# mLSTM stage of a hybrid encoder step: the decay mask as one product for four heads, the row values in two parts, and an end in which ScalarE normalizes while VectorE alternates two jobs

## The reference, cut to what matters

```
# per block of tokens and head: b = cumsum(log_sigmoid(f)), causal mask
dmat  = where(causal, b[t] - b[s] + ig[s], -inf)
m_t   = max(b + m, max_s dmat)
wqk   = exp(dmat - m_t) * (q @ k.T)                    # pair weights
num   = s_inter * (q @ c) + wqk @ v;  den likewise
h     = num / max(|den|, exp(-m_t))
c_new = s_old * c + (wg * k).T @ v                     # state, an output
# behind it, per token and head
hc    = (h - mean(h)) * rsqrt(var(h) + eps)            # headwise LayerNorm
yc    = hc * ml_norm_g * sigmoid(o)
```

## Time and profile before

| what | value |
|---|---|
| median of three runs | 2857.32 us (2831.56, 2857.32, 2858.39) |
| profiled execution | 2832.34 us |
| its span | 2830.6 us |
| TensorE busy in the span | 2560.8 us, 90% |
| VectorE, ScalarE, GpSimd busy | 1594.4, 1332.7, 649.7 us |
| `stage_mlstm` in the span | from 842.8 us; the next stage's first transfer is issued at 952.29 us |

### The profile page before, as it was taken

One profiled execution on the slowest core, in us unless ns is written; L12 is line 12 of the kernel. 1 busy time (PEld: TensorE's weight loads), 2 busy tenths in 40 slices (PEclk: granted clock), 3 DMA queues, 4 the chain that ended last, 5 costly groups with the idle time before them and its releaser, 6 DMA issues. The chain is left out here.

```text
span 2830.6 us, 40715 instructions
## 1 busy us (share of the span) xinstructions
PE 2560.8 (90%) x15168; PEld 2301.0 (81%) x15168; DVE 1594.4 (56%) x2533; ACT 1332.7 (47%) x2070; POOL 649.7 (23%) x508
## 2 busy tenths in 40 slices
PE   5999698998889699999989889699999999999990
PEld 4998597897658599999987567599999999999990
DVE  4564331216656644444534365577777777777774
ACT  3665420215433333434332222377777767777762
POOL 4000110004202001011113223134333343343333
PEclk8999899999999799999999889799999999999995
DMA  6120222213274655565534312689898898898964
GB/s 196 47 55 26 91 77 88 90 49 119 83 288 122 132 132 149 145 163 135 141 100 154 118 44 69 198 273 273 245 277 264 259 276 250 268 274 252 272 192 159
DMA packets 390447, 463.27 MB, mean 164 GB/s; under 512 B 21661, under 2 KB 314645, under 8 KB 390330
## 3 DMA queue, kind: packets, MB, share of 16 engines
q1 hardware_dynamic: 369160, 395.81, 45.4%
q0 software_dynamic: 16832, 55.62, 8.2%
q10 hardware_dynamic: 4338, 10.23, 0.9%
HBM read 397.62 MB, written 63.98 MB: 163 GB/s over the span
## 5 line engine op out<-in xcount | busy, mean ns | idle before, releaser
L3102 PE MATMUL banks<-slot_rowsT,expert_w_high 128*128 128x384 f32 x2048 | 604.2, 363 | 0.2 <-issue 0.2
L3104 PE MATMUL banks<-slot_rowsT,expert_w_low 128*128 128x192 f32 x2048 | 515.4, 252 | 0.0
L3104 PEld LDWEIGHTS banks<-slot_rowsT,expert_w_low 128*128 128x128 f32 x2048 | 392.9, 192 | 1.3
L3102 PEld LDWEIGHTS banks<-slot_rowsT,expert_w_high 128*128 128x128 f32 x2048 | 386.1, 189 | 2.0 <-issue 0.6
L3138 ACT CAST expert_w_high<-expert_w 128x2048 fp32r<-128x2048 f32 x128 | 238.1, 1910 | 20.5 <-DMA expert_w<-in_exp_w 20.5
L3197 DVE TENSOR_TENSOR expert_w_low<-expert_w,expert_w_high 128x2048 fp32r<-128x2048 f32 x96 | 216.7, 2284 | 20.8 <-ACT expert_w_high L3138 20.8
L3007 POOL TENSOR_TENSOR expert_w_low<-expert_w,expert_w_high 128x2048 fp32r<-128x2048 f32 x32 | 147.7, 4615 | 273.7 <-ACT expert_w_high L3138 273.7
L2050 PE MATMUL banks<-xT_chunk_high,w_gates_high 128*128 128x384 f32 x576 | 193.5, 336 | 15.0 <-DVE xT_chunk_low L2118 15.0
L2051 PE MATMUL banks<-xT_chunk_low,w_gates_high 128*128 128x384 f32 x576 | 193.2, 335 | 0.0
L2052 PE MATMUL banks<-xT_chunk_high,w_gates_low 128*128 128x384 f32 x576 | 193.1, 335 | 0.0
L3263 DVE TENSOR_TENSOR expert_w_low<-expert_w,expert_w_high 128x1024 fp32r<-128x1024 f32 x128 | 157.5, 1231 | 54.0 <-ACT expert_w_high L3167 54.0
(11 more groups left out here) (494 smaller groups left out, 6164.9 us busy)
## 6 DMA issues: line engine op xcount, KB each, us to landing
expert_w<-in_exp_w SPq DMA_DIRECT2D x128, 1024.0 KB, 8.9
expert_w<-in_exp_w SPq DMA_DIRECT2D x32, 2048.0 KB, 10.9
w_gates<-in_w_in SPq DMA_DIRECT2D x72, 512.0 KB, 4.5
cached_k<-in_cache_sb_k SPq DMA_DIRECT2D x16, 1024.0 KB, 8.3
cached_v<-in_cache_sb_v SPq DMA_DIRECT2D x16, 1024.0 KB, 9.9
w_proj<-in_w_pa SPq DMA_DIRECT2D x24, 512.0 KB, 5.1
w_ax_ag<-in_w_in SPq DMA_DIRECT2D x16, 512.0 KB, 5.1
w_ml_piece<-in_w_in SPq DMA_DIRECT2D x24, 256.0 KB, 4.0
```

Source lines behind the costliest of these rows:

```text
L3102: nc.tensor.matmul(out[:, 0:2 * SLOTS], hi, xgT[:, par, k].rearrange("p a s -> p (a s)"), start=(k == 0), stop=(k == DT - 1), skip_group_c ...
L3104: last = nc.tensor.matmul(out[:, 0:SLOTS], lo, xgT[:, par, k, 0, :], start=False, stop=(k == DT - 1), skip_group_check=True)
```

## The change

Four things change, all in `stage_mlstm`.

1. The mask. The causal masks are laid out once for four heads (`masks`, 128 x 512) in the one-pass type F32R, the identity is copied to that type too, and one product of 512 columns writes the mask of all heads into bank 0.
2. The row values. `m.w` is split into a high part (rows 0 to 3 of `w_rows`) and the remainder (rows 32 to 35), the selector is copied to both places, and one one-pass product of 36 rows per head adds both parts.
3. What that needs first: two clearing operations and a subtraction on VectorE, six copies on ScalarE, and waits of TensorE's first product for them.
4. The end. The normalization is ScalarE's (scale `rstd`, bias `shift` = -mean * rstd); variance and eps come before the requests' states; VectorE alternates a request's state and a tile's o gate, and TensorE alternates a request's products and a tile's transposes, in steps `s`, the gate and the transposes three steps behind.

```diff
+        w_rows = sb("w_row_parts", [L, T], F32R)              # L = 32 + H
+        sel = sb("head_selector_parts", [L, H, P], F32R)
+        ident = sb("ident_one_pass", [P, P], F32R)
+        masks = sb("causal_by_head", [P, 2, H, P], F32R)
...
         # TensorE, scores(i)
+                else:
+                    pe.wait_ge(masks_ready, 3)
+                    pe.wait_ge(parts_ready, 1)
+                nc.tensor.matmul(g.bank[0][:], ident[:], mask.rearrange("p h t -> p (h t)"), start=True, stop=False,
+                                 skip_group_check=True)
                 for h in range(H):
-                    out = g.bank[0][:, h * P:(h + 1) * P]
-                    nc.tensor.matmul(out, g.sel[:, h, :], m.w[:, cols], start=True, stop=False)
-                    last = nc.tensor.matmul(out, g.ident[:], mask[:], start=False, stop=True)
+                    last = nc.tensor.matmul(g.bank[0][:, h * P:(h + 1) * P], sel[:, h, :], w_rows[:, cols],
+                                            start=False, stop=(h == H - 1), skip_group_check=True)
...
         # TensorE, the end (request_state(b) is the loop body of before, turn_yc(i) the transposes)
+            for s in range(NT + 3):
+                if s < NB:
+                    request_state(s)
+                if s >= 3:
+                    turn_yc(s - 3)
...
         # ScalarE, first
+            act.wait_ge(parts_zero, 2)
+            for lo in (0, 32):
+                nc.scalar.copy(sel[lo:lo + H], g.sel[:])
+            nc.scalar.copy(w_rows[0:H], m.w[:]).then_inc(parts_high, 1)
+            nc.scalar.copy(ident[:], g.ident[:]).then_inc(masks_ready, 1)
+            for a, mask in enumerate((g.causal, g.causal_s)):
+                nc.scalar.copy(masks[:, a], mask[:].unsqueeze(1).broadcast_to([P, H, P])).then_inc(masks_ready, 1)
...
         # ScalarE, the end (move_yc(i) waits for yc_turned and copies to ycT, as before)
+            act.wait_ge(std_ready, 2)
+            for i in range(NT):
+                for h in range(H):
+                    part = hc[:, i, h * P:(h + 1) * P]
+                    last = nc.scalar.activation(part, part, ACT.Identity, bias=shift[:, i, h, :],
+                                                scale=rstd[:, i, h, :])
+                last.then_inc(hat_ready, 1)
+                if i >= 3:
+                    move_yc(i - 3)
...
         # VectorE, first; the old clearing of m.qz stands between these two and the subtraction
+            nc.vector.memset(sel[:].bitcast(F32), 0.0).then_inc(parts_zero, 1)
+            nc.vector.memset(w_rows[:].bitcast(F32), 0.0).then_inc(parts_zero, 1)
...
+            dve.wait_ge(parts_high, 1)
+            nc.vector.tensor_tensor(w_rows[32:32 + H], m.w[:], w_rows[0:H].bitcast(F32), ALU.subtract
+                                    ).then_inc(parts_ready, 1)
...
         # VectorE, the end
+            def gate_rows(i):
+                dve.wait_ge(hat_ready, i + 1)
...
+            for s in range(NT + 3):
+                if s == 1:
+                    dve.wait_ge(std_ready, 1)
+                    link(nc.vector.reciprocal(rstd[:], rstd[:]))
+                    nc.vector.scalar_tensor_tensor(out=shift[:], in0=mv[:, :, :, 0:1], scalar=-1.0, in1=rstd[:],
+                                                   op0=ALU.mult, op1=ALU.mult).then_inc(std_ready, 1)
+                if s < NB:
+                    request_state(s)
+                if s >= 3:
+                    gate_rows(s - 3)
```

More of the change, by code:

```diff
@@ L1640, in stage_mlstm, with sb @@
         sem = ctx.enter_context(stage_semaphores(nc))
-        def sb(name, shape):
-            return ctx.enter_context(nc.sbuf_tensor(name, shape, F32))
+        def sb(name, shape, dt=F32):
+            return ctx.enter_context(nc.sbuf_tensor(name, shape, dt))
+        L = 32 + H
+        w_rows = sb("w_row_parts", [L, T], F32R)
+        sel = sb("head_selector_parts", [L, H, P], F32R)
+        ident = sb("ident_one_pass", [P, P], F32R)
+        masks = sb("causal_by_head", [P, 2, H, P], F32R)
+        parts_zero = sem("r_parts_zero")
+        parts_high = sem("r_parts_high")
+        parts_ready = sem("r_parts_ready")
+        masks_ready = sem("r_masks_ready")
+        hat_ready = sem("r_hat_ready")
         c_state = sb("c_state", [P, 2, A])
@@ L1657, in stage_mlstm @@
         rstd = sb("hc_rstd", [P, NT, H, 1])
+        shift = sb("hc_shift", [P, NT, H, 1])
         seg = sb("request_mask", [P, NB])
@@ L1771, in scores @@
                 cols = slice(i * P, (i + 1) * P)
[L1772 removed]
+                mask = masks[:, 1 if i == NT - 1 else 0]
                 if i:
                     pe.wait_ge(dexp_ready, i)
+                else:
[3 more added lines that the diff above has]
+                                 skip_group_check=True)
                 for h in range(H):
[L1777 to L1779 removed]
+                    last = nc.tensor.matmul(g.bank[0][:, h * P:(h + 1) * P], sel[:, h, :], w_rows[:, cols],
+                                            start=False, stop=(h == H - 1), skip_group_check=True)
                 last.then_inc(w_bank, 1)
@@ L1837, in _, with request_state @@
             pe.wait_ge(inter_ready, NT)
-            for b in range(NB):
+            def request_state(b):
                 if b == 0:
@@ L1849, in _, with turn_yc @@
                 last.then_inc(c_prod, 1)
-            for i in range(NT):
+            def turn_yc(i):
                 pe.wait_ge(yc_ready, i + 1)
@@ L1877, in _, with move_yc @@
             nc.scalar.activation(rstd[:], mv[:, :, :, 1:2], ACT.Sqrt).then_inc(std_ready, 1)
-            for i in range(NT):
+            def move_yc(i):
                 act.wait_ge(yc_turned, i + 1)
@@ L1881, in _ @@
                                g.bank[2 + i % 2][:].rearrange("p (h t) -> p h t", h=H)).then_inc(yc_moved, 1)
+            act.wait_ge(std_ready, 2)
[7 more added lines that the diff above has]
+                    move_yc(i - 3)
+            for i in range(NT - 3, NT):
+                move_yc(i)
         @block.vector
@@ L1939, in _, with request_state @@
                     link(last)
-            for b in range(NB):
+            nc.vector.tensor_scalar(mv[:, :, :, 1:2], mv[:, :, :, 1:2], LN_EPS, None, ALU.add).then_inc(var_ready, 1)
+            def request_state(b):
                 dve.wait_ge(c_prod, 8 + b + 1)
                 new_state(cs[:, b], 8 + b, (6, 0)[b % 2])
[L1943 to L1950, removed]
-                link(last)
+            def gate_rows(i):
+                dve.wait_ge(hat_ready, i + 1)
                 if i == 0:
```

## The result

The changed kernel took 2866.64 us (median of 16 runs, 2843.18 to 2873.14), the kernel before 2836.47 in as many (2831.56 to 2858.87): a ratio of 1.0078, 95% interval 1.0059 to 1.0098. So it is slower, by 30 us (1.1%) in the medians and by 0.8% in the ratio, which goes by all runs. The two differ because both kernels fall into two groups of runs some 20 us apart, and a median jumps from one to the other when half of the runs do. Of the kernel before 5 of 16 are in the upper one (over 2850), of the changed kernel 12 of 16 (over 2865). The profiled executions, 2832.34 before and 2867.48 after, are one of either group, and their difference of 35.1 us has four parts: -3.1 ahead of the mLSTM stage, **+14.2 in it**, **+21.0 in the routing stage**, which the change does not touch, and +3.0 in the rest.

What follows compares the result with a forecast made beforehand. TensorE was taken to bound the loop, and the sample stores' start the stage's end. Opening +1.5, loop -3.5 and end +14.5 gave +12.5 us (+6 to +17), on 2857.32 a median of 2870 us, range 2838 to 2876.

Steps and rivals of the forecast that it cites:

- The ring: Stage end: TensorE and VectorE wait on each other in turn, 4.97 us a step (3.97 at full clock); end costs +14.5 us.
- The rule on transposes: Stage end: transposes do not bring up TensorE's full clock, so steps were taken at 0.50; full clock would give +10.5 us.
- The landing: Stage close: sample stores start at 943.9, land 19.9 us later at 963.8, and SyncE is last by 10 us or more.
- landing hidden: Rival, stage close: later stores land much faster, ScalarE's last copy ends the stage at about 952, sum about +1; chance 0.06.
- The opening: Stage start to first `num`: added clears, subtraction and the first tile's mask cost +1.5 us, between 0 and +5.
- The loop: Tiles between first and eighth `num`: shorter mask product cuts the period from 6.91 to 6.41 us, -3.5 us in all.
- seven such periods: Loop: the period of 6.41 instead of 6.91 us holds seven times, giving -3.5 us.
- the loop falls to half clock: Rival, loop: 2 us of idleness per tile drops TensorE to 0.50; +34.5 us in all, 2892 us; chance 0.08.
- 0.69 busy held 1.00: Loop: evidence against half clock; a profile row only 0.69 busy held full clock, and the loop keeps 4.4 of 6.4 us.
- The median: Whole kernel: forecast median 2870 us, from 2857.32 + 12.5.
- the upper level: Whole kernel: the runs shown lie at two levels 26 us apart; the upper, 2857.32 and 2858.39, sets the median.
- no row tells why: Whole kernel: no profile row was found to explain the two levels of runs, 26 us apart.

Runs made afterwards that it cites:

- products_ahead: Changed kernel with TensorE issuing the products of request s+1, not s, ahead of the transposes of tile s-3; 2841.37 us, ratio 1.0025.
- states_first: Changed kernel with all request states before all gates on VectorE, and TensorE and ScalarE likewise one job after the other; 2856.19 us, ratio 1.0024.
- mask_thrice: Changed kernel with the one-pass mask product issued three times from the second tile on; 2869.91 and 2871.82 us in two runs.
- fill_four_pass: Changed kernel with four plain fp32 products of 128 columns ahead of the one-pass mask product from the second tile on; 2846.62 us in one run.
- before_paced: Kernel before with the routing stage's indirect writes spread over TensorE's units by one wait; 2832.53 us, ratio 0.9963.
- after_paced: Changed kernel with the routing stage's indirect writes spread over TensorE's units by one wait; 2845.52 us, ratio 1.0016.
- mask_only: Changed kernel's mask and row values with the end as in the kernel before; 2852.98 us, ratio 1.0020.
- end_only: Kernel before with the change's new end alone, masks and row values as before; 2866.88 us, ratio 1.0077.
- scatter_late: Changed kernel with GpSimd's 36 indirect writes in the routing stage starting only after TensorE's tenth of eighteen units; 2870.93 us, ratio 1.0102.

## Why the prediction was right, and where it was not

- **The ring: confirmed.** That TensorE's products for a request stand behind transposes that wait for a gate of the same step was read from the order of the rows, and products_ahead, which changes that order alone, brings the step from 4.0 to 5.1 us down to 2.2. The steps were forecast at 4.97 or 3.97 us by the clock; both occurred: half clock in two steps (5.09), full clock in one (4.00), and the first (4.55) began at full clock. That is 1.15 of the 1.3 us by which the end came out cheaper.
- **The rule on transposes.** The Trainium skill (TensorE: Matmul & The Clock Gate, Part 4: PE-mode transpose) says that they do not bring up the full clock. The trace of the kernel before agrees, and the ring, which is no clean test because it mixes transposes with products, was at 1.00 once, from 932.0 to 935.0. But states_first does not agree: with transposes alone its clock rose from 0.50 to 1.00 at 941.6. As a basis for taking half clock in the ring the rule was not safe.
- **The landing: confirmed.** SyncE was last by 12.8 us, and the store started at 942.26, that is 945.4 on before's scale (943.9 forecast: the loop gave back 2.5 us less, the end cost 1.3 less). The rival "landing hidden" is out.
- **The opening: right**, +1.8 for +1.5. The mask began 8.55 us after the first clear (8.0 forecast) and took 1.74 us (1.5).
- **The loop: right in kind, mis-sized.** The step that failed is "seven such periods". The period is 6.46 for 6.41 (0.4 us in seven), the seventh is 7.00 because VectorE's `den` and `hc` took 0.5 us longer, while GpSimd masked k (in the kernel before 0.1; no run isolates why), and one tile falls to half clock (1.5). The rival "the loop falls to half clock" took place in one tile of seven, not in all. "0.69 busy held 1.00" was no evidence for this loop: that row held plain fp32 products alone. The Trainium skill (the same page, A second HAM failure mode: psum-queue depth-cycling) names micro-idles that let the clock swing; the runs agree that it swings (one tile in seven, and every second in mask_thrice), yet less idle time went with more of it in mask_thrice and with none in fill_four_pass.
- **The median: near by luck.** The forecast of 2870 was "the upper level" of three runs plus 12.5 us. The kernel before is at the lower level in most runs, so its median is 2836.47, and the change was 30 us, not 12.5. The step "no row tells why" stood for a stage that I had not read. Some 13 us are the change's own price (before_paced beside after_paced), the rest comes from being in the upper group more often. Why the changed kernel is there in 12 of 16 runs and the kernel before in 21 of 93 is open: the four kernels between them that keep the writes unspread (mask_only, end_only, products_ahead, states_first) are there in 23 of 40.

## What to carry to other kernels

When two engines alternate two jobs, write down for one step which instruction stands behind which wait on each queue; if each engine's second job waits for the other's first, they take turns, and the step is the sum of both. Put the work that others wait for one step ahead on the queue, and start transfers of many small pieces as soon as the first part is ready. When runs of one kernel fall into groups, find the stage that differs between two profiles before forecasting a median: here it was worth as much as the change.

## What the runs showed that I had not expected

- While GpSimd issues 36 indirect writes without a break (47 to 50 us), the issue of the other engines can slow down: in scatter_late TensorE's from one product per 0.23 us to one per 0.6 to 3.5 us, up to the end of the writes. It doesn't always: in the profile of the kernel before TensorE kept to 0.23 us beside the same writes. With the writes in short groups with rests, no run of the four paced kernels (33) is in an upper group, and before_paced is 0.37% faster. What else it takes is open. The Trainium skill (SBUF — State Buffer, SBUF: two separate sides, the "DVE blocks DMA" trap) tells of the other direction, VectorE's work keeping GpSimd from writing the descriptors of its transfers; no run here shows by what path the writes hold up TensorE.
- With 0.8 us more of plain fp32 products per tile TensorE's clock stayed at 1.00 through the loop (two profiles), with as much time in one-pass products it fell in every second tile (one profile): periods of 6.46 us beside 7.19 and 6.47 in turn.
- With transposes alone TensorE's clock stayed at 0.50 for 18.6 us in the kernel before (busy 10.04) and rose to 1.00 in states_first (busy 5.46 of 6.60 ahead of it).
- ScalarE normalizes a 128x512 tile in 1.65 us with a scale and bias per head, and moving that job to it cost nothing by itself: in states_first it closes 11 us ahead of the stores.
